# Seven block products for eight in a feed-forward layer: quarters two to four of the first product

## The reference

```
def channel_and_ple(h, p_i, g_pre, g_post, w_ff_in, w_ff_out, w_pg, w_pp):
    u = rmsnorm(h, g_pre)
    f = jnp.square(jax.nn.relu(u @ w_ff_in)) @ w_ff_out
    h = h + rmsnorm(f, g_post)
    return h + jax.nn.sigmoid(h @ w_pg) * (p_i @ w_pp)
```

## Time and profile before

| | us |
|---|---|
| median of three runs | 1658.39 |
| the three runs | 1665.58, 1656.79, 1658.39 |
| the profiled execution | 1658.19 |
| its span, first to last instruction | 1656.4 |
| TensorE busy in the span | 1598.9 |
| VectorE, ScalarE, POOL busy | 824.0, 647.7, 117.0 |

### The profile page before, as it was taken

One profiled execution on the slowest core, in us unless ns is written; L12 is line 12 of the kernel. 1 busy time (PEld: TensorE's weight loads), 2 busy tenths in 40 slices (PEclk: granted clock), 3 DMA queues, 4 the chain that ended last, 5 costly groups with the idle time before them and its releaser, 6 DMA issues.

```text
span 1656.4 us, 32232 instructions
## 1 busy us (share of the span) xinstructions
PE 1598.9 (97%) x13788; PEld 1481.4 (89%) x13788; DVE 824.0 (50%) x1091; ACT 647.7 (39%) x1141; POOL 117.0 (7%) x146
## 2 busy tenths in 40 slices
PE   8999899999999999999999879999999999999998
PEld 7787699999999999999999655566999999999998
DVE  6988537533333336733342566653464433334372
ACT  5434555323132333522233366764442322323242
POOL 1000000000000000010240352210000000000000
PEclk9999999999999999999999989999999999999999
DMA  7533152322222222321236300002222232322221
GB/s 201 154 103 113 36 190 71 102 83 96 88 92 78 90 88 77 102 84 54 74 115 207 119 1 1 1 15 77 78 83 95 78 102 77 102 77 89 90 77 55
DMA packets 139624, 145.69 MB, mean 88 GB/s; under 512 B 6563, under 2 KB 131315, under 8 KB 139280
## 3 DMA queue, kind: packets, MB, share of 16 engines
...
## 4 chain that ended last, share of the span: by engine, by line
PE 86%; DVE 7%; ACT 4%; issue 2%; DMA 1%; SPq 0%; POOL 0%; ACTq 0%; DVEq 0%
PE ps L389 63%; PE ps L522 2%; PE ps L1215 2%; PE ps L1064 2%; PE ps L1063 2%; PE ps L1065 2%; PE ps L1742 2%; PE ps L1720 2%; DVE w_lo L374 1%; PE ps L1721 1%; PE ps L575 1%; PE ps L1663 1%; ACT w_hi L369 1%; PE ps L1664 1%; DVE resid L688 1%
## 5 line engine op out<-in xcount | busy, mean ns | idle before, releaser
L389 PE MATMUL ps<-x_hi,w_hi 128*128 128x272 f32 x1664 | 361.1, 290 | 11.3 <-DVE x_lo L2535 4.3
L389 PE MATMUL ps<-x_hi,w_lo 128*128 128x272 f32 x1664 | 358.0, 289 | 0.0
L389 PE MATMUL ps<-x_lo,w_hi 128*128 128x272 f32 x1664 | 356.9, 288 | 0.0
L374 DVE TENSOR_TENSOR w_lo<-w_raw,w_hi 128x2048 fp32r<-128x2048 f32 x101 | 233.8, 2315 | 141.5 <-ACT w_hi L369 139.6
L369 ACT ACTIVATE w_hi<-w_raw 128x2048 fp32r<-128x2048 f32 x101 | 192.7, 1908 | 267.8 <-PE ps L389 265.0
L389 PEld LDWEIGHTS ps<-x_hi,w_hi 128*128 128x128 f32 x1664 | 267.1, 189 | 20.3 <-issue 11.6
L389 PE MATMUL ps<-hid_hi,w_hi 128*128 128x272 f32 x1280 | 268.0, 289 | 2.2 <-DVE hid_lo L2043 1.5
L389 PE MATMUL ps<-hid_hi,w_lo 128*128 128x272 f32 x1280 | 267.4, 288 | 0.0
L389 PEld LDWEIGHTS ps<-x_lo,w_hi 128*128 128x128 f32 x1664 | 267.4, 189 | 0.0
L389 PE MATMUL ps<-hid_lo,w_hi 128*128 128x272 f32 x1280 | 266.6, 288 | 0.0
L389 PEld LDWEIGHTS ps<-x_hi,w_lo 128*128 128x128 f32 x1664 | 265.7, 189 | 0.0
...
## 6 DMA issues: line engine op xcount, KB each, us to landing
w_raw<-in_ffn_w_in SPq DMA_DIRECT2D x64, 512.0 KB, 4.6
w_raw<-in_ffn_w_out SPq DMA_DIRECT2D x64, 512.0 KB, 4.3
w_raw<-in_nsa_w_in SPq DMA_DIRECT2D x20, 512.0 KB, 4.6
w_raw<-in_ple_w_gate SPq DMA_DIRECT2D x16, 512.0 KB, 4.4
w_raw<-in_conv_w_in SPq DMA_DIRECT2D x15, 512.0 KB, 5.6
w_raw<-in_conv_w_out SPq DMA_DIRECT2D x8, 512.0 KB, 4.0
w_raw<-in_nsa_w_o SPq DMA_DIRECT2D x8, 512.0 KB, 4.7
...
```

Of the source, the lines that this page charges most:

```text
L374: dve.tensor_tensor(WL[par][:, :], RAW[par][:, :], WH[par][:, :].bitcast(F32), ALU.subtract)\
L389: m = pe.matmul(o_, w[par][:, wcols:wcols + P], x[:, k, c_], start=f, stop=l)
```

## The change

Quarters two to four of the first product are done by a scheme of seven block products in place of eight (Strassen-Winograd, one level). The weight block of a unit (1,024 x 512) is cut into four blocks a, b, c, d of 512 x 256, the tokens into four blocks of 512 features x 272 columns. From the weights come four sums per unit: s3 = a + c, s2 = s3 + d, s4 = s2 + b on VectorE, s1 = c + d on POOL. The token sums (`T2`, `N3`, `N1`, `N4`) are made once a layer while quarter one's second product runs (`turn_x_act`, `turn_x_dve`). A quarter has two units (u = 0, 1) of seven products (i = 0 to 6), each of 24 matmuls.

Each engine has a new list. ScalarE (`fast_act`) makes the high part of a half slab two products ahead (`fast_hi`), copies product 0 out of PSUM, and turns each quad of hidden values (two chunks by one token half) by relu, square and copy (`quad_act`). VectorE (`fast_dve`) makes low parts (`fast_lo`), the sums, and seven evictions per unit (`evict_dve`). POOL (`fast_pool`) makes s1 and the low parts of the quads. `g_full` counts products, `g_dve` evictions, `g_hi` and `g_lo` high and low parts, `g_sum` VectorE's sums, `g_s1` POOL's.

New tiles lie over others: `sum_v`, `sum_w` and one raw half slab over the constants, which SP loads a second time in layer 0. The per-layer input's rows now lie over `x_hi`, so `load_p` waits for all products of a layer and comes behind `fast_pool`; their transposes stand in quarter four's second product. The all-ones matmuls stand ahead of quarter two. The loops over quarters two and three are written out. The core of the diff:

```
+        HALF = SLAB // 2
+        (VACC, WACC, W_E), e = over(cst_at + 2 * P * 4, ("sum_v", [P, 2, HT], F32), ("sum_w", [P, 2, HT], F32), ("w_raw_e", [P, HALF], F32))
...
+        (W_Z,), _ = over(z_at, ("w_sum_z", [P, HALF], F32))
...
+        OPS, UNITS, PRODS = 15, 2, 7
...
+        def raw_slots(p0, u):
+
+            r = [w_half(RAW, p0, i) for i in range(4)]
+            return (r[0], r[1], r[2], r[3], W_Z[:, :]) if u == 0 else (W_E[:, :], r[2], r[0], r[3], W_Z[:, :])
+
+        def raw_of(p0, u, i):
+
+            a_, b_, c_, d_, z_ = raw_slots(p0, u)
+            return (a_, a_, b_, z_, c_, d_, b_)[i]
...
+        FAST_BANK = (0, 4, 0, 2, 6, 2, 6)
+        QUADS = ((0, A_, 1.0), (2, B_, -1.0), (2, A_, -1.0), (0, B_, 1.0))
...
+        def fast_pe(pe, l, q, s0, b0):
+
+            g0 = OPS * (3 * l + q - 1)
+            b_e = b0 + 8 + 8 * q
+            for u in range(UNITS):
+                un = UNITS * (3 * l + q - 1) + u
+                for i in range(PRODS):
+                    if i == 0:
+                        pe.wait_ge(S["g_dve"], NC + max(7 * un - 5, 0))
+                        if u == 0:
+                            pe.wait_ge(blk_free, b_e - 1)
+                    elif i == 1:
+                        pe.wait_ge(S["g_dve"], NC + max(7 * un - 6, 0))
+                        if q == 1 and u == 0:
+                            pe.wait_ge(S["stat_used"], (4, 8)[l])
+                            pe.wait_ge(S["t_lo"], 4 * l + 1)
+                    elif i == 2:
+                        pe.wait_ge(S["g_act"], un + 1)
+                        pe.wait_ge(S["g_dve"], NC + 7 * un + 1)
+                    elif i == 3:
+                        pe.wait_ge(S["g_dve"], NC + max(7 * un - 1, 0))
+                        if u == 0:
+                            pe.wait_ge(blk_free, b_e)
+                        if q == 1 and u == 0:
+                            pe.wait_ge(S["t_lo"], 4 * l + 2)
+                    elif i == 4:
+                        pe.wait_ge(S["g_dve"], NC + 7 * un)
+                        if q == 1 and u == 0:
+                            pe.wait_ge(S["t_lo"], 4 * l + 3)
+                    elif i == 5:
+                        pe.wait_ge(S["g_dve"], NC + 7 * un + 3)
+                        if q == 1 and u == 0:
+                            pe.wait_ge(S["t_lo"], 4 * l + 4)
+                    else:
+                        pe.wait_ge(S["g_dve"], NC + 7 * un + 5)
+                    pe.wait_ge(S["g_lo"], NC + g0 + PRODS * u + i + 1)
+                    wh, wl = [w_half(w, s0 % 2, fast_slot(i)) for w in (WH, WL)]
+                    hi, lo = FAST_X[i]
+                    for mb in range(2):
+                        out = PS[:, FAST_BANK[i] + mb, 0:HT]
+                        for k in range(4):
+                            c = slice(k * NSLABCOL + mb * P, k * NSLABCOL + (mb + 1) * P)
+                            pe.matmul(out, wh[:, c], hi(k), start=k == 0, stop=False)
+                            pe.matmul(out, wh[:, c], lo(k), start=False, stop=False)
+                            m = pe.matmul(out, wl[:, c], hi(k), start=False, stop=k == 3)
+                    m.then_inc(S["g_full"], 1)
...
+        def fast_hi(act, l, q, s0, b0, u, i):
+
+            p0, un = s0 % 2, UNITS * (3 * l + q - 1) + u
+            if i in (0, 2, 5):
+                raw_waits(act, l, q, u, {0: "a", 2: "b", 5: "d"}[i])
+            else:
+                act.wait_ge(*((S["g_s1"], NC // 2 + un + 1) if i == 4 else (S["g_sum"], 3 * un + {1: 2, 3: 1, 6: 3}[i])))
+            fast_before(act, l, q, b0, u, i)
+            act.activation(w_half(WH, p0, fast_slot(i)), raw_of(p0, u, i), ACT.Copy).then_inc(S["g_hi"], 1)
+
+        def fast_lo(dve, L, l, q, s0, u, i):
+
+            p0, n = s0 % 2, OPS * (3 * l + q - 1) + PRODS * u + i
+            dve.wait_ge(S["g_hi"], NC + n + 1)
+            L(dve.tensor_tensor(w_half(WL, p0, fast_slot(i)), raw_of(p0, u, i), w_half(WH, p0, fast_slot(i)).bitcast(F32), ALU.subtract),
+              S["g_lo"], wait=False)
+
+        def fast_sums(dve, L, l, q, s0, u, which):
+
+            a_, b_, c_, d_, z_ = raw_slots(s0 % 2, u)
+            n, un = OPS * (3 * l + q - 1) + PRODS * u, UNITS * (3 * l + q - 1) + u
+            if which == "s3":
+                raw_waits(dve, l, q, u, "ac")
+                L(dve.tensor_tensor(z_, a_, c_, ALU.add), S["g_sum"])
+            elif which == "s2":
+                raw_waits(dve, l, q, u, "d")
+                dve.wait_ge(S["g_lo"], NC + n + 1)
+                L(dve.tensor_tensor(a_, z_, d_, ALU.add), S["g_sum"])
+            else:
+                dve.wait_ge(S["g_lo"], NC + n + 3)
+                L(dve.tensor_tensor(b_, a_, b_, ALU.add), S["g_sum"], wait=False)
...
+        def quad_act(act, L, l, q, u, n):
+
+            un, h = UNITS * (3 * l + q - 1) + u, 8 * (4 * l + q) + 4 * u
+            rows, c = hid_cols(l, q, u, n)
+            act.wait_ge(S["g_dve"], NC + 7 * un + (2, 4, 6, 7)[n])
+            L(act.activation(TMP[n][:, :], TMP[n][:, :], ACT.Relu, scale=QUADS[n][2]))
+            L(act.activation(TMP[n][:, :], TMP[n][:, :], ACT.Square))
+            L(act.activation(HH[:, rows, c], two(TMP[n][:, :]), ACT.Copy), S["hid_hi"], wait=False)
+
+        def quad_pool(pool, L, l, q, u, n):
+
+            h = 8 * (4 * l + q) + 4 * u + n
+            rows, c = hid_cols(l, q, u, n)
+            pool.wait_ge(S["hid_hi"], h + 1)
+            L(pool.tensor_tensor(HL[:, rows, c], two(TMP[n][:, :]), HH[:, rows, c].bitcast(F32), ALU.subtract), S["h_ready"], wait=False)
+
+        def fast_pool(pool, L, l, s0):
+
+            for q in range(1, 4):
+                for u in range(UNITS):
+                    c_, d_ = raw_slots(s0 % 2, u)[2:4]
+                    pool.wait_ge(S["g_sum"], 3 * (UNITS * (3 * l + q - 1) + u) + 2)
+                    L(pool.tensor_tensor(c_, c_, d_, ALU.add), S["g_s1"], wait=False)
+                    for n in range(4):
+                        quad_pool(pool, L, l, q, u, n)
+
+        def evict_dve(dve, L, l, q, u, n):
+
+            un, h = UNITS * (3 * l + q - 1) + u, 8 * (4 * l + q) + 4 * u
+            full = PRODS * un
+            dve.wait_ge(S["g_full"], NC + full + (2, 3, 4, 5, 5, 6, 7)[n])
+            if n == 0:
+                dve.wait_ge(S["g_act"], un + 1)
+                L(dve.tensor_tensor(VACC[:, :, :], two(TMP[0][:, :]), PS[:, 4:6, 0:HT], ALU.subtract), S["g_dve"])
+            elif n == 1:
+                L(dve.tensor_tensor(two(TMP[0][:, :]), PS[:, 0:2, 0:HT], two(TMP[0][:, :]), ALU.add), S["g_dve"], wait=False)
+            elif n == 2:
+                L(dve.tensor_tensor(WACC[:, :, :], VACC[:, :, :], PS[:, 2:4, 0:HT], ALU.subtract), S["g_dve"])
+            elif n == 4:
+                L(dve.tensor_tensor(VACC[:, :, :], PS[:, 6:8, 0:HT], VACC[:, :, :], ALU.add), S["g_dve"])
+            else:
+                x = {3: 1, 5: 2, 6: 3}[n]
+                dve.wait_ge(S["h_ready"], h - 3 + x if u or q > 1 else h)
+                out = two(TMP[x][:, :])
+                if n == 3:
+                    L(dve.tensor_tensor(out, PS[:, 6:8, 0:HT], WACC[:, :, :], ALU.add), S["g_dve"], wait=False)
+                elif n == 5:
+                    L(dve.tensor_tensor(out, WACC[:, :, :], PS[:, 2:4, 0:HT], ALU.subtract), S["g_dve"], wait=False)
+                else:
+                    L(dve.tensor_tensor(out, PS[:, 6:8, 0:HT], VACC[:, :, :], ALU.add), S["g_dve"], wait=False)
+
+        def fast_act(act, L, l, q, s0, b0):
+
+            for n in range(2 * PRODS):
+                u, i = n // PRODS, n % PRODS
+                un = UNITS * (3 * l + q - 1) + u
+                if i == 1:
+                    act.wait_ge(S["g_full"], NC + PRODS * un + 1)
+                    act.wait_ge(S["h_ready"], 8 * (4 * l + q) + 4 * u - (3 if u or q > 1 else 0))
+                    L(act.activation(two(TMP[0][:, :]), PS[:, 0:2, 0:HT], ACT.Copy), S["g_act"], wait=False)
+                if n + 2 < 2 * PRODS:
+                    fast_hi(act, l, q, s0, b0, (n + 2) // PRODS, (n + 2) % PRODS)
+                elif n + 2 == 2 * PRODS:
+                    first_half_hi(act, l, q, s0)
+                else:
+                    second_half_hi(act, l, q, s0)
+                if i in (3, 5, 6):
+                    quad_act(act, L, l, q, u, {3: 0, 5: 1, 6: 2}[i])
+                elif n == PRODS:
+                    quad_act(act, L, l, q, 0, 3)
+            quad_act(act, L, l, q, 1, 3)
+
+        def fast_dve(dve, L, l, q, s0, b0):
+
+            for n in range(2 * PRODS):
+                u, i = n // PRODS, n % PRODS
+                for e in {2: (0,), 3: (1,), 4: (2,), 5: (3, 4), 6: (5,)}.get(i, ()):
+                    evict_dve(dve, L, l, q, u, e)
+                if n == PRODS:
+                    evict_dve(dve, L, l, q, 0, 6)
+                if n + 2 < 2 * PRODS:
+                    fast_lo(dve, L, l, q, s0, (n + 2) // PRODS, (n + 2) % PRODS)
+                elif n + 2 == 2 * PRODS:
```

(92 more changed lines are left out.)

365 lines of the change are left out of this document (240 added, 125 removed).

## The result

The changed kernel takes 1694.13 us (median of four runs, 1693.30 to 1694.92), beside 1657.72 for the kernel before in the same session. The ratio is 1.021, with a 95% interval of 1.0183 to 1.0238. It is slower, as forecast, but by 36.4 us and not by 18; the range ended at 1688. The profiled spans are 1693.0 and 1656.4 us.

What follows compares the result with a forecast made beforehand. TensorE's matmuls were taken to bound the kernel, with the order of work deciding. Stops and clock drops less 18.06 us saved gave +12.6 or +5.7 per layer; twice their middle, +18.2 on 1658.2, gave 1676 us, range 1651 to 1688.

Steps and rivals of the forecast that it cites:

- POOL first: Unit 0 to unit 1: POOL's block sum precedes low half 3, which waits 2.3 us more; +12.6 us per layer.
- VectorE first: Unit 0 to unit 1: low half 3 precedes POOL's block sum; stop 3.73 us, +5.7 us per layer.
- the first two places: TensorE waits before product 2: 1.05 us in first units, 3.7 or 6.0 us from unit 0 to unit 1.
- the third: Start of quarter two: TensorE waits 1.47 us before product 0 and 3.1 before product 1, 4.57 us per layer.
- The port rival: VectorE and POOL: sharing the port costs nothing because operations happen to pass each other; 1651.5 us, chance 0.10.
- the rival of a covered chain: Unit 0 to unit 1: the 14.8 us chain shrinks by 2.8 and stays covered by 12.04 us; 1641 us, chance 0.14.
- VectorE as the bound: All units: POOL's 7.9 us falls on VectorE's 17.2, 25.1 us against 21.1; 1680 to 1700 us, chance 0.06.
- So the stop is 3.7 or 6.0 us: Unit 0 to unit 1: TensorE's stop, shorter with VectorE ahead, longer with POOL ahead; which is more frequent left open.
- A stop of 6.0 us will cost 1.6 us more: Behind the unit boundary: TensorE's clock drops to 1.2 GHz after the stop, 1.6 us more per boundary.
- The low end for 3.7 us, no fall: Behind the shorter boundary stop: clock cost taken as 1.6 us, with 0 as lower end if the clock holds.
- the top of its range: 1688 us: POOL ahead at every boundary, with the 3.1 us stop at quarter two's start dropping the clock as well.
- What the prediction put at nothing: Token sums, weight loads, `load_p`, transposes, all-ones matmuls, reloaded constants and the second product's first block: hidden, no time added.

Runs made afterwards that it cites:

- e2: Changed kernel with POOL's block sum s1 of second units waiting until VectorE's low half 3 is done: 1680.56 us, ratio 1.0128 to the kernel before.
- e1: Changed kernel without product 2's wait for eviction 0: 1659.62 us, ratio 0.9985 to the kernel before.
- e3: Changed kernel with quarter two's first two low halves, s3 and s2 ahead of quarter one's last two evictions: 1679.83 us, ratio 1.0117 to the kernel before.
- e6: Changed kernel with s3 of the second unit one step earlier in VectorE's list: 1684.33 us, ratio 1.0124 to the kernel before.
- e4: Changed kernel with the edits of e1, e3 and e6 together: 1638.06 us, ratio 0.9867 to the kernel before.
- e5: Changed kernel with 40 unused matmuls per second unit ahead of the wait for eviction 0: 1680.88 us, ratio 1.0114 to the kernel before.

## Why the prediction was wrong in size

**Right: the places, and their order.** TensorE stops exactly where the prediction put it. In first units the distance from product 1's last matmul (364.11) to product 2 (365.26), less one pitch of 0.125, is 1.02 us (predicted 1.05). At the boundary it is 392.08 - 386.31 - 0.13 = 5.64 (6.03 with POOL first); with VectorE first, in e2, 387.92 - 384.23 - 0.13 = 3.56 (3.73). At the start of quarter two the two stops are idle times of 1.32 and 2.68 and, with 0.16 each for the modelled ends, 4.3 us (4.57). e1 takes the first two places out but for short stops, e3 the third, and e6 shortens the boundary's stop by the link that it takes out. The port rival is refuted by e2, the rival of a covered chain by the changed kernel itself, and VectorE as the bound by e1 and e4.

**Wrong: "So the stop is 3.7 or 6.0 us", taken at the middle.** The prediction had the two outcomes within 0.05 us and averaged them over the six boundaries. But both engines follow fixed lists and the same chain at every boundary, and the outcome was one for all six, in both traces of the changed kernel: POOL leads by 0.11 or 0.12 us every time. A middle between the two outcomes did not occur; the sum should have been +12.6 per layer (1683.4) or +5.7 (1669.6), with a chance for each. This is 6.9 us of the miss.

**Wrong size: the clock.** "A stop of 6.0 us will cost 1.6 us more" came from a single row pair. Here it cost 2.6 at the first boundary and 2.2 in the mean of six (e5), some 4 us in all. The low end for 3.7 us, no fall, did not occur: after 3.4 us the clock fell six times out of six (e2). And the clock fell at the start of quarter two in three of the four cases of the changed kernel's two traces, which the prediction had only in the top of its range.

**Wrong: the base, and no room for the unchanged stages.** What the prediction put at nothing did cost nothing: no stop of TensorE in these parts is put down to a load, and e4 keeps 25 us with all the moved loads, sums and transposes in place. But the sum was taken against one profiled execution whose clock fell little (1658.19 us, where 15 later runs of the same kernel have a median of 1661.81), and had no term for what the unchanged stages take from run to run. They came out 7.3 us longer in the first trace and 4.7 in the second, against that execution; the kernel before's later medians lie 3.6 to 5.7 us above it. That the clock has a part in it is shown for the stretch above; why it falls more often in one execution than in another is not settled. The four runs of the changed kernel lie within 1.6 us, while e4 has much the same code and only +1.4, in a trace of the fastest of its five runs.

By its own terms, with measured sizes: 3 x (1.02 + 5.64 + 2.2) + 4.3 - 18.06 = +12.8 per layer, 0.6 for eight restarts (the second matmul behind a stop comes 0.20 us after the first, not 0.125) and 1.5 where the clock fell at the start: 13.4 to 14.9, beside 14.3 to 15.9 in the traces. Up to 1 us per layer is not placed.

The Trainium skill (SBUF - State Buffer, SBUF: two separate sides) says that of a vector operation with two SBUF inputs and a POOL operation that reads SBUF the one that starts first has their shared port for its whole duration. The trace agrees: low half 3, 1.22 us alone, ends 1.09 us after POOL's sum, which started 0.12 us ahead of it. The Trainium skill (GPSIMD Engine Reference, Performance versus the Vector engine) gives 4,497 ns for 2,048 columns; the estimate of 2.25 us for that sum, half of it, is a little low: it measured 2.34 to 2.39.
